# Boundaries between sublayers, passed by token tile instead of by column half

## The reference

```
first block, for each of 2 layers:
    x = x + rms_norm(mixer(rms_norm(x, g0)), g1)              # even: fox + nsa attention; odd: differential
    x = x + rms_norm(memory_attention(rms_norm(x, g2)), g3)
    x = x + rms_norm(swiglu(rms_norm(x, g4)), g5)             # 1024 -> 2816 -> 1024
second block, for each of 2 layers:
    x = x + 0.5 * swiglu(rms_norm(x, n1))
    z = rms_norm(x, n2) @ w_in
    mixed = gates * three branches(z)
    x = x + mixed @ w_out
    x = x + 0.5 * swiglu(rms_norm(x, n3))
```

## Time and profile before

| what | us |
|---|---|
| median of 3 runs | 2318.67 |
| lowest, highest | 2317.66, 2322.11 |
| the profiled execution's own time | 2311.67 |
| its span in the trace | 2309.7 |
| PE busy | 2098.5 (91%) |
| DVE busy | 1249.0 (54%) |
| ACT busy | 1022.5 (44%) |
| POOL busy | 139.7 (6%) |
| mean granted PE clock | 0.951 of full |

### The profile page before, as it was taken

How to read it: one execution, slowest core, us unless ns; L and a number is a source line. 1 busy time by engine, 2 the same in 40 slices (tenths; PEclk the granted TensorE clock), 3 DMA queues, 4 the chain that set the end, 5 groups by cost and what they waited for, 6 DMA issues and landing times.

```text
span 2309.7 us, 26412 instructions
## 1 busy us (share of the span) xinstructions
PE 2098.5 (91%) x9932; PEld 1709.9 (74%) x9932; DVE 1249.0 (54%) x1669; ACT 1022.5 (44%) x1501; POOL 139.7 (6%) x134
## 2 busy tenths in 40 slices
PE   6977789989869998999989699999999989879998
PEld 6764678877658887887767568887887767657887
DVE  3735455456655555545656645445545565565554
ACT  4534344445444444344444454444444445444433
POOL 0000000000000000000302300000000211211000
PEclk8977899999979999999899799999999999989999
DMA  8421246554225554554532435555555443424552
GB/s 269 125 75 44 92 158 197 183 167 137 62 100 185 194 186 152 194 182 160 159 128 77 139 108 182 183 192 171 183 186 178 139 142 114 155 70 150 189 193 91
DMA packets 247748, 346.11 MB, mean 150 GB/s; under 512 B 28292, under 2 KB 177608, under 8 KB 247624
## 3 DMA queue, kind: packets, MB, share of 16 engines
q1 hardware_dynamic: 245816, 340.37, 45.7%
q10 hardware_dynamic: 1264, 2.79, 0.4%
q0 software_dynamic: 544, 1.29, 0.2%
HBM read 343.35 MB, written 2.33 MB: 150 GB/s over the span
## 4 chain that ended last, share of the span: by engine, by line
PE 79%; issue 8%; DVE 6%; ACT 3%; POOL 2%; DMA 1%; DVEq 0%; ACTq 0%; SPq 0%; POOLq 0%
PE bank L622 24%; PE bank L624 23%; PE bank L623 23%; PE bank L960 1%; PE bank L1141 1%; PE bank L851 1%; POOL o_buf L2159 1%; PE bank L557 1%; ACT w_hi L469 1%; PE bank L1010 1%; ACT h_hi L597 1%; DMA raw<-in_ev_w_in 1%; DVE w_lo L457 1%; DVE x L1306 1%; DVE jobstat L884 1%
## 5 line engine op out<-in xcount | busy, mean ns | idle before, releaser
L457 DVE TENSOR_TENSOR w_lo<-raw,w_hi 128x2048 fp32r<-128x2048 f32 (+5 forms) x447 | 739.0, 1665 | 466.2 <-ACT w_hi L469 465.6
L622 PE MATMUL bank<-w_hi,h_hi 128*128 128x512 f32 (+4 forms) x1936 | 771.8, 399 | 75.1 <-DVE w_lo L457 39.9
L624 PE MATMUL bank<-w_hi,h_lo 128*128 128x512 f32 (+4 forms) x1936 | 757.2, 391 | 0.0
L623 PE MATMUL bank<-w_lo,h_hi 128*128 128x512 f32 (+4 forms) x1936 | 756.5, 391 | 0.0
L469 ACT CAST w_hi<-raw 128x2048 fp32r<-128x2048 f32 (+5 forms) x447 | 616.5, 1396 | 313.8 <-PE bank L624 295.3
L622 PEld LDWEIGHTS bank<-w_hi,h_hi 128*128 128x128 f32 x1936 | 376.6, 195 | 161.0 <-issue 52.0
L624 PEld LDWEIGHTS bank<-w_hi,h_lo 128*128 128x128 f32 x1936 | 375.8, 194 | 72.6
L623 PEld LDWEIGHTS bank<-w_lo,h_hi 128*128 128x128 f32 x1936 | 377.1, 195 | 67.0
L622 PE MATMUL bank<-w_hi,ff_hi 128*128 128x512 f32 x528 | 206.1, 390 | 0.0
L624 PE MATMUL bank<-w_hi,ff_lo 128*128 128x512 f32 x528 | 205.6, 389 | 0.0
L623 PE MATMUL bank<-w_lo,ff_hi 128*128 128x512 f32 x528 | 205.4, 389 | 0.0
(11 more groups left out here) (258 smaller groups left out, 1593.2 us busy)
## 6 DMA issues: line engine op xcount, KB each, us to landing
raw<-in_ffn_w SPq DMA_DIRECT2D x176, 512.0 KB, 4.5
raw<-in_w_in SPq DMA_DIRECT2D x52, 1024.0 KB, 5.2
raw<-in_ffn_w SPq DMA_DIRECT2D x44, 1024.0 KB, 4.9
raw<-in_ffn_wg SPq DMA_DIRECT2D x44, 512.0 KB, 4.0
raw<-in_ffn_wu SPq DMA_DIRECT2D x44, 512.0 KB, 5.0
raw<-in_ffn_wd SPq DMA_DIRECT2D x22, 1024.0 KB, 4.9
raw<-in_od_w_in SPq DMA_DIRECT2D x12, 1024.0 KB, 5.1
raw<-in_w_out SPq DMA_DIRECT2D x8, 1024.0 KB, 5.1
```

The costliest lines, as they stand in the source:

```text
L457: dve.tensor_tensor(lo_[:, cs], raw_[:, cs], hi[:, cs].bitcast(F32), ALU.subtract).then_inc(*dve_did.up())
L622: pe.matmul(out, x_hi, u.hi[:, k, cols_], start=start, stop=False)
L623: pe.matmul(out, x_hi, u.lo[:, k, cols_], start=False, stop=False)
L624: return pe.matmul(out, x_lo, u.hi[:, k, cols_], start=False, stop=stop)
```

## The change

All boundaries are passed token tile by token tile:

- `pre_norm` transposes tile 0 (blocks 0 to 3, then 4 to 7) and then tile 1. A bank now holds four blocks of one tile, evacuated in four pieces of 128 columns. ACT waits for `start.dve`, all that DVE was given before. The result is a `ByTile`: ready by tile and half.
- The last products of a sublayer are issued for tile 0 first: `out_steps` in its second half, `gemm_by_tile` for memory attention's wo, `last_down` for the FFN.
- `Sublayer` takes the power and adds to x for each tile (`summed`, `finish(tt)`), so a POOL power comes twice.
- The first chunk of the next GEMM, or of the FFN, takes both its units first and then goes through tile 0 with both, then tile 1 with both.
- w_out of the second block comes in units of the two halves of the inner dimension. Its first half is multiplied for both column chunks before the second half of o_buf is transposed.
- The output leaves in four transfers by tile and half instead of two.

The core of the diff:

```diff
-        units += gemm_units(a["w_out_2"][l], chunked(D))
+        units += half_units(a["w_out_2"][l], 0) + half_units(a["w_out_2"][l], KD // 2)
...
+                if isinstance(ready, ByTile) and c == chunks[0][0]:
+                    whole = []
+                    while k0 < nk:
+                        whole.append((k0, take()))
+                        k0 += whole[-1][1].shape[0]
+                    for tt in range(TT):
+                        for k0, u in whole:
+                            yield from tile_steps(tt, h, k0, u, nk, c, n, pair, ready.upto(tt, k0 + u.shape[0]), evac)
+                    continue
...
+        def gemm_by_tile(h, nk, chunks, evac, ready):
...
+            for tt in range(TT):
+                for c, n, pair, u in whole:
+                    for _ in tile_steps(tt, h, 0, u, nk, c, n, pair, ready, evac):
+                        pass
...
+            first = [take(), take()]
+            for tt in range(TT):
+                gate_up(0, first[0], 0, [tt])
+                gate_up(0, first[1], KD // 2, [tt])
+                hidden(0, [tt])
+            for c in range(1, NF + 1):
...
-            for half in range(2):
-                for tt in range(TT):
-                    finish(tt, half, acc[tt * 2 + half], pe_did.now())
+            u = take()
+            for tt in range(TT):
+                last_down(u, tt)
...
-                            ready=lambda b: x_ready[k0 // HALF], after=start)
+            for tt in range(TT):
+                ts_ = slice(tt * P, (tt + 1) * P)
+                for half in range(2):
+                    bank, k0 = next_bank(), half * HALF
...
+                        pe.wait_ge(*x_ready[tt][half])
+                        for b in range(HALF):
+                            m = pe.transpose(bank.t[:, b * P:(b + 1) * P], src[:, tt, (k0 + b) * P:(k0 + b + 1) * P], ident)
...
+                        act.wait_ge(*full)
+                        act.wait_ge(*start.dve)
+                        for b in range(HALF):
+                            act.activation(h_hi[:, k0 + b, ts_], bank.t[:, b * P:(b + 1) * P], ACT.Copy,
+                                           scale=gains[b]).then_inc(*act_did.up())
...
-                if half == 0:
-                    self.multiply(tt, c, bank, self.squared)
-                else:
-                    self.last.append((tt, c, bank, self.squared))
+                if half == 1:
+                    self.summed(tt)
+                self.multiply(tt, c, bank, self.squared)
+                if half == 1:
+                    self.finish(tt)
...
+            both = [(c, take()) for c in (0, 512)]
+            for tt in range(TT):
+                for c, u in both:
+                    yield from tile_steps(tt, h, k0, u, KD, c, 512, acc[c], ready, leave)
...
-            gemm(h_in, KD, chunked(D), add_x, halves_of_o(marks_of=by_half))
+            acc = out_banks()
+            for k0, after in zip((0, KD // 2), by_half):
+                groups, steps = half_of_o(k0, after)
+                for _ in steps:
+                    pass
+                for _ in out_steps(acc, h_in, k0, groups[-1], add_x):
+                    pass
```

More of the change, by code:

```diff
@@ new lines, in tile_steps, with _ @@
+            ts_ = slice(tt * P, (tt + 1) * P)
+            for ka in range(0, kk, step):
+                last = ka + step == kk
+                @block.tensor
+                def _(pe):
+                    if ka == 0 and there is not None:
+                        pe.wait_ge(*there.act)
+                        pe.wait_ge(*there.dve)
+                    if k0 == 0 and ka == 0:
+                        pe.wait_ge(*pair[tt].drained)
+                    pe.wait_ge(*u.parted)
+                    for k in range(ka, ka + step):
+                        m = three_products(pe, pair[tt].t[:, 0:n], h[0][at + k][:, ts_], h[1][at + k][:, ts_],
+                                           u, k, slice(0, n), k0 + k == 0, k0 + k == nk - 1)
+                    if last:
+                        m.then_inc(*pe_did.up())
+                if last and tt == TT - 1:
+                    u.used = pe_did.now()
+                    u.at = turn["steps"]
+                if last and k0 + kk == nk:
+                    pair[tt].held = False
+                    evac(tt, c, n, pair[tt], pe_did.now())
+                yield True
@@ L732, in rstd_rows @@
             start = start or marks()
[L733 removed]
+            src_ready = src_ready or [start.dve] * TT
             @block.scalar
@@ L1229, in program @@
+            rstd_rows(src, r, start, [x_ready[tt][1] for tt in range(TT)])
+            squares_read["x"] = act_did.now()
+            return ByTile(there)
         gain_used = [const_landed.now()] * 2
```

203 lines of the change are left out of this document (104 added, 99 removed).

## The result

| | before | after |
|---|---|---|
| median of six runs, us | 2318.16 | 2332.48 |
| lowest and highest | 2312.22, 2323.74 | 2328.14, 2336.61 |
| profiled run, its span | 2311.67, 2309.7 | 2331.37, 2329.6 |

What follows compares the result with a forecast made beforehand. PE was taken to bound the kernel, with the stretches around sublayer boundaries and the granted clock next. Terms summed to +3.2 us, +7.7 with the clock, added to the 2318.67 median: 2326.4 us, range 2314 to 2334.

Steps and rivals of the forecast that it cites:

- FFN to next, second block: Three boundaries: two x operations instead of four left after the last product, so the next GEMM starts earlier; 4.5 us saved.
- FFN to next, first block: Two boundaries: less DVE work behind the w_lo subtraction, so h_hi starts earlier, and a smaller first bank; 4.2 us saved.
- mixer to memory: Two boundaries: one multiply and two x go, and the GEMM wants tile 0's blocks only; 4.8 us saved.
- memory to FFN: Two boundaries: earlier h_hi, but the second unit's CAST falls behind the norm; 2.4 us lost and 1.0 saved, 1.4 lost.
- w_out to FFN, stall: Two places: PE idles over 5 us after tile 0's first quarter for the second unit's w_lo; 4.8 us lost each.
- stop in w_out: Middle of w_out's products, twice: PE waits for the second half's transposes, h_hi and h_lo; 2.7 us lost each.
- start: First chunk of the kernel: three quarters instead of two are left when the second unit is there; 1.5 us lost.
- end: Before the last output transfer: two x operations instead of four; 1.2 us saved.
- clock: Half clock after four stalls: 1.5 us each at w_out to FFN, 0.75 each at memory to FFN; 4.5 lost.
- Rival 2: Stalls as forecast, but small evacuations at their lower bound and the clock stays up: around 2318 us; chance 0.22.
- Rival 3: Fourth unit's CAST waits behind tile 1's evacuation; eight boundaries lose 0.5 to 1 us: 2334 us; chance 0.08.
- Rival 1: Splits don't hold PE, the second unit's w_lo being ready after tile 0's first quarter: 15.1 us faster, 2303.6; chance 0.10.

Runs made afterwards that it cites:

- e_wout: Changed kernel, but in w_out of the second block both halves of o_buf are transposed and evacuated ahead of the first product; 2318.4 us, 1.0009 of the kernel before.
- e_split: Changed kernel with the second gate/up unit's CAST ahead of the norm and its w_lo mid-norm, at four places before an FFN; 2309.7 us, 0.9968 of the kernel before.
- e_fix: Changed kernel with the edits of e_split and e_wout, and the very first GEMM's first chunk unit by unit; 2296.0 us, 0.9903 of the kernel before.
- e_bank: Changed kernel with the bank counter set to 4 before the norm from memory attention to FFN; 2331.8 us, 1.0065 of the kernel before.
- e_only_early: Changed kernel, but ACT's h_hi of tile 0 doesn't wait for tile 1's last x, except in the first norm; 2309.2 us, 0.9963 of the kernel before.
- e_nofill: e_early without the fillers, that is e_fix with ACT's early h_hi; 2277.5 us, 0.9836 of the kernel before.
- e_warm: Changed kernel with idle transposes of the identity keeping TensorE busy in every norm but the first; 2314.5 us, 1.0000 of the kernel before.
- e_best: e_fix with fillers on TensorE as in e_warm, but fewer at the short gaps of the second block; 2291.4 us, 0.9881 of the kernel before.
- e_early: e_best, but ACT's h_hi of tile 0 no longer waits for tile 1's last x, except in the first norm; 2272.9 us, 0.9808 of the kernel before.
- e_final: e_early with the bank counter of e_bank; 2265.2 us, 0.9787 of the kernel before.

## Why the prediction was right, and where it was not

Measured is after less before in the two profiles, from T to e where nothing else is said.

| step | predicted | gaps | first chunks | together |
|---|---|---|---|---|
| FFN to next, second block (7, 9, 10) | -4.5 | -4.5 | +4.8 | +0.3 |
| FFN to next, first block (3, 6) | -4.2 | -4.6 | +4.1 | -0.5 |
| mixer to memory (1, 4) | -4.8 | -5.2 | -0.5 | -5.7 |
| memory to FFN (2, 5) | +1.4 | -6.0 | +8.7 | +2.7 |
| w_out to FFN, stall (8, 11) | +9.6 | -0.9 | +15.1 | +14.2 |
| stop in w_out (its length) | +5.4 | | | +5.3 |
| start | +1.5 | | | +6.0 |
| end (T to the span's end) | -1.2 | | | -1.8 |
| clock | +4.5 | | in the rows above | |
| mixers and the rest between, less the stop | 0 | | | -0.4 |
| sum | +7.7 | | | +19.9 |

The direction, the stall at w_out and the terms of the gaps were right. ACT's first h_hi did wait for tile 1's last x, and the gaps forecast as 3.9, 7.5 and 7.6 us came out at 3.8 to 4.1, 7.3 and 7.35. Sixteen h_hi took 4.23 us (4.27 said), at 415 ns each, h_lo 343, squares 1172. That DVE w_lo would hold PE one quarter into the chunk was seen at all four places; the two at w_out gave 5.04 and 5.02, the forecast "over 5". But the sign asked for over 4 us at four places, and memory to FFN gave 0.56 and 2.57. There w_lo was ready 14.0 and 14.3 us behind T (14.5 said), but the first quarter took 5.5 us at half clock and not 2.75, and so used up most of the wait. The stop in w_out was 2.65 for 2.7. It is read from its own rows: the whole stretches that hold it (e of place 7 to T of 8, and of 10 to 11) were 0.1 and 1.6 us shorter than before.

```profile
L1298 ACT ACTIVATE h_hi<-bank,cols 128x128 fp32r<-128x128 f32 x192 | 50.8, 415 | 56.6 <-DVE x L2714 22.2 <-DVE x L1392 13.1 <-DVE x L1266 9.8
L1305 DVE SCALAR_TENSOR_TENSOR h_lo<-bank,cols,h_hi 128x128 fp32r<-128x128 f32 x192 | 50.7, 343 | 16.8 <-ACT h_hi L1298 16.8
```

**The step that failed is the clock.** I put 4.5 us on it, at four stalls, and nothing on the shortened boundaries, with the reason "after 5.3 us with transposes in them it cost nothing". That read the row by its length, and took a shorter gap for a safe one. The change also moved the transposes and the stops inside the gaps, and with them the time of half clock. At places 3, 6, 7, 9 and 10, where I had 0, the chunks grew by 8.9 us, and at 8 and 11 5.0 lay behind the stall instead of 3. At place 5 the chunk grew by 7.0, of which 2.57 were idle. In all it was 18.9 us instead of 4.5. There was no row of the clock at FFN to mixer in the prediction; before, there was half clock in that gap too (492.20 to 498.90 above), but it fell on idle time and transposes.
TensorE: Matmul & The Clock Gate of the Trainium skill (Part 1) says that throttled is the default and that activity releases it. The stalls at 8 and 11 agree, with 5.0 us. At 7, 9 and 10 that sentence alone would not have given it: at place 7 PE was idle for 3.2 us of the gap before and for 2.0 after, and the three chunks grew by 4.8 us all the same.

**The start** was mis-sized: 6.0 for 1.5. Over the seven profiles with tile order at the start e lies at 35.7 to 40.0, mean 37.8; over the seven with unit order, the kernel before among them, at 32.4 to 35.9, mean 34.4. So 3.4 is the estimate of the effect from these profiles, and the rest goes with when the first weights' data came. In the changed kernel's profile w_lo of the second unit ran at 28.90, in e_wout's, the same code there, at 25.65.

**How errors met.** Between the profiles the clock was 14.4 us dearer than said and the start 4.5. Against that memory to FFN came out 4.2 better without its clock (gaps -6.0, idle +3.1, where +1.4 was said), and the other terms 2.3 better together. Between the medians the miss is 6.6 us and not 12.2, because the profile of before is 6.5 under its median. So the number was nearer than its parts, and that is luck: the forecast range was met near its upper end with a clock term four times too small. Rival 2 (the clock stays up) fell. Rival 3's price of 2334 was nearly met, by another cause. Rival 1 was wrong here, but e_split shows that its direction was right for a kernel whose splits are in time.

What stays open: what decides whether the clock falls at places 7, 9 and 10. And within the mixers and the projection the clock falls and rises at other places in each profile (with the same code there, e of place 10 to T of place 11 is 313 to 323 us). The -0.4 of the table hides such swings: +2.6 and +2.5 us in the two mixers of the first block, +1.6 in its first memory attention, -2.7 and -4.3 in the stretches that end with w_out. No run here ties them to the change.

## What to carry to other kernels

When a change shortens waits, ask for each place not only when PE's next product can start but what PE does in the gap ahead of it, and when: half clock that lies in idle time is free, and the same half clock moved onto the first products cost 1.6 us at a place behind gaps of 4 and 2 us behind gaps of 7. A shorter gap can so lose what it saved. Look at the granted clock in the gap and behind it apart; the mean over the program (0.951 and 0.949) hardly showed it. Passing data on tile by tile pays only if no engine in the chain still waits for the whole; here one wait on ACT held back some 19 us, and without it the changed kernel is 0.4% faster than the one before. And when a finer order wants the next weights sooner, look where their splitting stands in the queues of ACT and DVE, since that place is set by when slots come free, not by when the data is wanted.

## What the runs showed of the hardware

- The granted clock can fall behind a gap in which it was 1.00 throughout. At place 7 PE worked 2.09 of 4.10 us in the gap, and the 4 us behind it had 0.59; with the same instructions and the same gaps, 4 of 15 such chunks at places 7, 9 and 10 (after, e_split, e_wout, e_fix, e_bank) kept 1.00.
- Gaps of 3.27 us at places 8 and 11 with the 16 transposes at their start and a stop of 1.52 us kept the clock at the first products in 10 of 10 cases (the same five kernels), and gaps of 2.9 us at 7, 9 and 10 in 6 of 6 (e_only_early, e_nofill).
- Short transposes of the identity in the gap (e_warm, e_best, e_early, e_final) gave full clock to 20 of 20 chunks at places 3, 6, 7, 9 and 10, behind gaps of up to 7.3 us.
- Half the columns cost far more than half the time: one evacuation takes 415 ns for 128 against 482 for 256 on ACT, and 16 of the small ones take 4.23 us against 3.03 for 8 of the large.
- A bank of the first product can be one that still holds the other tile's transposes; the trace then names h_lo as the releaser, and only the twelfth of 16 fits the time (307.35 worked out, 307.40 seen; with another bank the gap fell from 7.96 to 5.99).
